# Reading a gate straight from PSUM, and writing each head's decay work in one piece, in a 25,527-instruction block kernel

## The reference, cut to what matters

```python
def second_block(x, ...):
    u = rmsnorm(h, norm_mix[l])                 # 272 tokens: 16 meta + 256
    proj = u @ w_in[l]                          # 1024 -> 6160 columns
    y_ssd = ssd_branch(z, xbc, dt_raw, ...)
    y_sc = short_conv_branch(gate_b, gate_c, h, conv_w, norm_g)
    h = h + jnp.concatenate([y_ssd, y_sc], axis=-1) @ w_out[l]
    ...                                         # router and experts

def short_conv_branch(gate_b, gate_c, h, conv_w, norm_g):
    v = causal_dwconv(gate_c * h, conv_w)
    return group_rmsnorm(gate_b * v, norm_g, SC_GROUPS)

def ssd_chunked(xs, dt, A, Bm, Cm):             # per head, chunks of 128 tokens
    seg = A_cum[..., :, None] - A_cum[..., None, :]
    Lmat = jnp.exp(jnp.where(causal, seg, -jnp.inf))
    CB = jnp.einsum('bcqgn,bckgn->bcgqk', Cc, Bc)
    y_diag = jnp.einsum('bcgqk,bcgrqk,bckgrp->bcqgrp', CB, Lmat, xdt)
    ...                                         # states carried over chunks, and y_off
```

## Time and profile before

| what | value |
|---|---|
| median of three runs | 1582.92 us |
| the profiled execution's own time | 1585.08 us |
| its span in the profile | 1583.3 us |
| PE busy | 1516.9 us (96%) |
| DVE busy | 847.7 us (54%) |
| ACT busy | 736.1 us (46%) |
| the chain that ended last | PE 79%, DVE 8%, DMA 5%, ACT 5% |
| the changed stage | about 1182 to 1285 us |

### The profile page before, as it was taken

How to read it: one execution, slowest core, us unless ns; L and a number is a source line. 1 busy time by engine, 2 the same in 40 slices (tenths; PEclk the granted TensorE clock), 3 DMA queues, 4 the chain that set the end, 5 groups by cost and what they waited for, 6 DMA issues and landing times.

```text
span 1583.3 us, 25527 instructions
## 1 busy us (share of the span) xinstructions
PE 1516.9 (96%) x10510; PEld 1175.5 (74%) x10510; DVE 847.7 (54%) x1494; ACT 736.1 (46%) x1151; POOL 1.4 (0%) x6
## 2 busy tenths in 40 slices
PE   8999989999999999999999999999999989999986
PEld 5645668777787778879968899997988889544442
DVE  2446666744333444674497765666578765212213
ACT  3535562543322332363364754546555644555444
POOL 0000000000000000000000000000000000000000
PEclk9999999999999999999999999999999999999999
DMA  9411633344433442343302446543444336999995
GB/s 388 174 44 64 209 128 106 133 160 160 163 117 133 159 175 103 135 159 108 107 1 84 157 154 206 186 147 135 159 143 152 110 145 251 421 420 421 421 420 226
DMA packets 42777, 288.29 MB, mean 182 GB/s; under 512 B 4880, under 2 KB 5008, under 8 KB 11808
## 3 DMA queue, kind: packets, MB, share of 16 engines
q1 hardware_dynamic: 42336, 285.93, 48.0%
q0 software_dynamic: 176, 0.59, 0.1%
q10 hardware_dynamic: 144, 0.06, 0.0%
HBM read 285.51 MB, written 1.05 MB: 181 GB/s over the span
## 4 chain that ended last, share of the span: by engine, by line
PE 79%; DVE 8%; DMA 5%; ACT 5%; issue 2%; SPq 1%; DVEq 0%; ACTq 0%
PE ps L550 16%; PE ps L551 16%; PE ps L552 16%; PE ps L3006 6%; DMA deep<-wts 5%; PE ps L601 2%; ACT WH L525 2%; DVE WL L535 1%; PE ps L1483 1%; PE ps L1581 1%; PE ps L1552 1%; DVE X L2126 1%; PE ps L2882 1%; PE ps L1653 1%; PE ps L1652 1%
## 5 line engine op out<-in xcount | busy, mean ns | idle before, releaser
L535 DVE TENSOR_TENSOR WL<-ring,WH 128x2048 fp32r<-128x2048 f32 (+2 forms) x134 | 281.2, 2103 | 138.7 <-ACT WH L525 138.6
L550 PE MATMUL ps<-HH,WH 128*128 128x512 f32 (+2 forms) x944 | 325.6, 345 | 3.6 <-DVE WL L535 3.6
L551 PE MATMUL ps<-HL,WH 128*128 128x512 f32 (+2 forms) x944 | 320.6, 340 | 0.0
L552 PE MATMUL ps<-HH,WL 128*128 128x512 f32 (+2 forms) x944 | 320.5, 339 | 0.0
L525 ACT ACTIVATE WH<-ring 128x2048 fp32r<-128x2048 f32 (+2 forms) x134 | 236.1, 1764 | 168.4 <-PE ps L552 91.4
L550 PEld LDWEIGHTS ps<-HH,WH 128*128 128x128 f32 (+1 forms) x944 | 179.1, 190 | 43.8 <-issue 19.3
L552 PEld LDWEIGHTS ps<-HH,WL 128*128 128x128 f32 (+1 forms) x944 | 179.1, 190 | 20.3
L551 PEld LDWEIGHTS ps<-HL,WH 128*128 128x128 f32 (+1 forms) x944 | 179.3, 190 | 18.4
L550 PE MATMUL ps<-UHL,WH 128*128 128x256 f32 (+3 forms) x416 | 121.8, 293 | 6.2 <-ACT cst L2351 2.4
L550 PE MATMUL ps<-parts,WH 128*128 128x512 f32 (+1 forms) x352 | 119.1, 338 | 0.4 <-DVE WL L535 0.4
L551 PE MATMUL ps<-UHL,WH 128*128 128x256 f32 (+3 forms) x416 | 118.3, 284 | 0.0
(11 more groups left out here) (425 smaller groups left out, 2508.2 us busy)
## 6 DMA issues: line engine op xcount, KB each, us to landing
ring<-wts SPq DMA_DIRECT2D x138, 1024.0 KB, 5.0
deep<-wts SPq DMA_DIRECT2D x80, 1024.0 KB, 18.2
ring<-wts SPq DMA_DIRECT2D x32, 704.0 KB, 4.0
under_x<-wts SPq DMA_DIRECT2D x12, 1024.0 KB, 19.9
arena<-wts SPq DMA_DIRECT2D x8, 1024.0 KB, 15.2
ring<-wts SPq DMA_DIRECT2D x4, 672.0 KB, 13.4
X<-xin SPq DMA_DIRECT2D x4, 512.0 KB, 16.2
ahead<-wts SPq DMA_DIRECT2D x2, 1024.0 KB, 8.1
```

Source lines behind the costliest of these rows:

```text
L535: e.tensor_tensor(lo, raw(i), hi.bitcast(F32), ALU.subtract).then_inc(*up("low", i))
L550: e.matmul(o, w[0][:, cols], x[0], start=k == 0, stop=False)
L551: e.matmul(o, w[0][:, cols], x[1], start=False, stop=False)
L552: return e.matmul(o, w[1][:, cols], x[0], start=False, stop=k == nk - 1)
```

## The change

It has four parts.

1. ACT's copy of part 0 (L2178) goes. The last of DVE's five operations on a short-convolution tile reads part 0 in its PSUM bank instead.
2. The bank of part 0 is therefore given back with that operation (`sc_out`, x, 4), and in the list it stands behind the bank of part 2. All later banks are handed out in another order.
3. DVE's near and mix of one head are written in one piece (`dve_head_decay`), so a step is near of head i, mix of head i, out of head i - 2.
4. In ACT's and DVE's programs the split of a chunk stood between scan 2i - 1 and scan 2i. It now stands ahead of scan 2i - 1, for the chunk before that one, so that each chunk's split comes one scan later than it did.

```diff
 def act_sc_tile(e, f):
     x, part = divmod(f, 3)
-    if part == 0:
-        e.wait_ge(*win_done(24 + f))
-        e.activation(YC[:, x, :], B("win", 24 + f)[:, LATENT], ACT.Copy).then_inc(*up("sc_gate.kept", x))
-    elif part == 1:
+    if part == 1:
...
 # dve_sc_tile, last operation
-e.tensor_tensor(YC[:, x, :], CV[:, z, LATENT], YC[:, x, :], ALU.mult).then_inc(*up("sc_out", x, 4))
+e.tensor_tensor(YC[:, x, :], CV[:, z, LATENT], B("win", 24 + f - 2)[:, LATENT],
+                ALU.mult).then_inc(*up("sc_out", x, 4))
...
-def dve_head_near(e, h):
+def dve_head_decay(e, h):
...
-    e.tensor_scalar(EZ[:, 528:656], second, bc(2, 128), 0.0, ALU.add, ALU.min).then_inc(*up("head_mixed.near", h))
-
-def dve_head_mix(e, h):
-    EZ = EE[h % 4]
+    e.tensor_scalar(EZ[:, 528:656], b[:, 144:272], bc(2, 128), 0.0, ALU.add,
+                    ALU.min).then_inc(*up("head_mixed.near", h))
     e.wait_ge(*at("head_exp", h))
...
 # dve_scan
-    i = f - 5
-    if i < 16:
-        dve_head_near(e, i)
-    if 0 <= i - 1 < 16:
-        dve_head_mix(e, i - 1)
-    if 0 <= i - 2 < 16:
-        dve_head_out(e, i - 2)
+    step_heads(f - 5, lambda h: dve_head_decay(e, h), lambda h: dve_head_out(e, h))
...
 # pe_second_half
-banks.give(banks.of["win", 24 + f], *(("sc_gate.kept", x), ("sc_gate", x), ("sc_out", x, 0))[part])
+if part == 1:
+    banks.give(banks.of["win", 24 + f], "sc_gate", x)
+elif part == 2:
+    banks.give(banks.of["win", 24 + f], "sc_out", x, 0)
+    banks.give(banks.of["win", 24 + f - 2], "sc_out", x, 4)
...
 def dve_second_half(e):          # act_second_half likewise
-    dve_low(e, index["win", 12])
-    dve_win_tile(e, 22)
-    dve_win_tile(e, 23)
     for i in range(12):
-        if i:
-            dve_scan(e, 2 * i - 1)
-        if i < 11:
-            dve_low(e, index["win", 13 + i])
-        dve_scan(e, 2 * i)
+        dve_low(e, index["win", 12 + i])
+        if i == 0:
+            dve_win_tile(e, 22)
+            dve_win_tile(e, 23)
+        for f in (2 * i - 1, 2 * i):
+            if f >= 0:
+                dve_scan(e, f)
     dve_scan(e, 23)
```

More of the change, by code:

```diff
@@ L2338, in head_bias @@
             return lambda i, n: bias6[0:n, 16 * i + h:16 * i + h + 1]
-        def head_decays(h):
-            return B("head", h)[:, 16:144], B("head", h)[:, 144:272]
         def act_head_decay(e, h):
             EZ = EE[h % 4]
-            (first, second), bc = head_decays(h), head_bias(h)
+            b, bc = B("head", h), head_bias(h)
             e.wait_ge(*at("head_mixed.near", h))
@@ L2348, in act_head_decay @@
                 e.wait_ge(*at("head_out", h - 4))
-            e.activation(EZ[0:16, 16:144], first[0:16, :], ACT.Exp, bias=bc(3, 16), scale=1.0)
-            e.activation(EZ[0:16, 144:272], second[0:16, :], ACT.Exp, bias=bc(4, 16), scale=1.0)
-            e.activation(EZ[:, 400:528], second, ACT.Exp, bias=bc(5, 128), scale=1.0).then_inc(*up("head_exp.far", h))
+            e.activation(EZ[0:16, 16:144], b[0:16, 16:144], ACT.Exp, bias=bc(3, 16), scale=1.0)
+            e.activation(EZ[0:16, 144:272], b[0:16, 144:272], ACT.Exp, bias=bc(4, 16), scale=1.0)
+            e.activation(EZ[:, 400:528], b[:, 144:272], ACT.Exp, bias=bc(5, 128),
+                         scale=1.0).then_inc(*up("head_exp.far", h))
             e.activation(EZ[:, 272:400], EZ[:, 272:400], ACT.Exp)
             e.activation(EZ[:, 528:656], EZ[:, 528:656], ACT.Exp).then_inc(*up("head_exp", h))
-        def dve_head_near(e, h):
+        def dve_head_decay(e, h):
             EZ = EE[h % 4]
-            (first, second), bc = head_decays(h), head_bias(h)
+            b, bc = B("head", h), head_bias(h)
             e.wait_ge(*at("decay_bias"))
@@ L2361, in dve_head_near @@
                 e.wait_ge(*at("head_out", h - 4))
-            e.tensor_scalar(EZ[:, 272:400], first, bc(1, 128), 0.0, ALU.add, ALU.min)
-            e.tensor_scalar(EZ[:, 528:656], second, bc(2, 128), 0.0, ALU.add, ALU.min).then_inc(*up("head_mixed.near", h))
-        def dve_head_mix(e, h):
-            EZ = EE[h % 4]
+            e.tensor_scalar(EZ[:, 272:400], b[:, 16:144], bc(1, 128), 0.0, ALU.add, ALU.min)
+            e.tensor_scalar(EZ[:, 528:656], b[:, 144:272], bc(2, 128), 0.0, ALU.add,
+                            ALU.min).then_inc(*up("head_mixed.near", h))
             e.wait_ge(*at("head_exp", h))
@@ L2481, in pe_second_half @@
                         pe_scan(e, f - 1)
-                    banks.give(banks.of["win", 24 + f], *(("sc_gate.kept", x), ("sc_gate", x), ("sc_out", x, 0))[part])
+                    if part == 1:
[3 more added lines that the diff above has]
+                        banks.give(banks.of["win", 24 + f - 2], "sc_out", x, 4)
             pe_scan(e, 23)
         def act_second_half(e):
-            act_high(e, index["win", 12])
-            act_win_tile(e, 22)
-            act_win_tile(e, 23)
             for i in range(12):
-                if i:
-                    act_scan(e, 2 * i - 1)
-                if i < 11:
-                    act_high(e, index["win", 13 + i])
-                act_scan(e, 2 * i)
+                act_high(e, index["win", 12 + i])
+                if i == 0:
+                    act_win_tile(e, 22)
+                    act_win_tile(e, 23)
+                for f in (2 * i - 1, 2 * i):
+                    if f >= 0:
+                        act_scan(e, f)
             act_scan(e, 23)
         def dve_second_half(e):
-            dve_low(e, index["win", 12])
-            dve_win_tile(e, 22)
-            dve_win_tile(e, 23)
             for i in range(12):
-                if i:
-                    dve_scan(e, 2 * i - 1)
-                if i < 11:
-                    dve_low(e, index["win", 13 + i])
-                dve_scan(e, 2 * i)
+                dve_low(e, index["win", 12 + i])
+                if i == 0:
+                    dve_win_tile(e, 22)
+                    dve_win_tile(e, 23)
+                for f in (2 * i - 1, 2 * i):
+                    if f >= 0:
+                        dve_scan(e, f)
             dve_scan(e, 23)
```

## The result

The changed kernel took 1593.96 us (median of 8 runs, 1589.9 to 1598.95) against 1584.0 (8 runs, 1580.3 to 1590.27) for the kernel before on the same chip. The ratio is 1.006 with a 95% interval of 1.0045 to 1.0077: slower by 0.6%, an estimated 7 to 12 us. The forecast was 1591.6 us, +8.7. The profiled execution of the changed kernel took 1596.89 us, its span is 1595.1.

A forecast was written before the change was run, and what follows sets the result against it. PE bounds the stage before; the change makes DVE the bound. Terms of -0.4, +7.5 and +1.6 give +8.7 us on 1582.9, so 1591.6 us; own range 1587 to 1595, 8 times in 10 1586.5 to 1597.

The forecast's parts named there:

- the forecast's mechanism: In the head steps DVE waits for ACT's exponentials between near and mix and becomes the bound; chance 0.76.
- Parts 1 and 2 cost nothing: DVE's last short-convolution multiply reading PSUM costs 0, later banks cost 0, and PE's 1.63 us stop at tile 3 goes.
- the wait of 1.42 a head: Between near and mix DVE waits 1.42 us per head; six scans take DVE 30.0 us against PE's 25.7.
- Part 4 uses slack in the middle: Later splits use only slack mid-stage; near the end the root comes earlier and one DVE split moves into the tail.
- first rival: The wait fits in DVE's air and PE's two stops go: 5.7 us won, 1577.2 us; chance 0.07.
- PE is stopped from tile 12: PE's first long stop is 1.9 us at column tile 12; from there PE follows DVE.
- It goes through to the end: What the stage gains or loses reaches the kernel's end, the expert stage keeping its length.
- second rival: The stage grows, but the experts' weight load at 420 GB/s takes it up: 1582.9 us; chance 0.05.
- third rival: PE's clock falls at about five new stops, 1.7 us each: +8.5 more, 1600.1 us; chance 0.12.
- The 1.7 us that the prediction read from the mean of 0.79: Loss from PE's slow clock over 8 us after the 2.39 us stop ahead of tile 23: 0.21 x 8 = 1.7 us.
- The sum: Along DVE's program: start -0.4, near 0 to near 15 +7.5, near 15 to output projection +1.6; together +8.7 us.
- bounds of -2.4 and +7: Effect on the sum over 16 heads if the wait between near and mix is at least 1.27 or at most 1.9 us.

The follow-up runs named there:

- two exponentials fewer: Changed kernel without ACT's last two exponentials of every head: 2733.87 us, including an expert branch at the end that the other kernels don't enter.
- out between near and mix: Changed kernel with out of head i - 2 placed between near and mix of head i on DVE: 1589.98 us, ratio 1.0021 against before.
- longer exponentials: Three of ACT's five exponentials per head split into halves, in the changed kernel (1597.7 us, ratio 1.0089) and in the kernel before (1584.98 us, 0.9999).
- part 3 alone: Kernel before with only near and mix of a head put in one piece on DVE: 1592.62 us, ratio 1.0057.
- DVE's splits as before: Changed kernel with DVE's splits back where they stood, ACT's still one scan later: 1602.46 us, ratio 1.0121 against before.
- parts 1 and 2 alone: Kernel before with only ACT's copy of part 0 gone and its bank given back later: 1585.68 us, ratio 1.0003.
- part 4 alone: Kernel before with only ACT's and DVE's splits one scan later: 1581.14 us, ratio 0.9986.
- ACT's half alone: Kernel before with only ACT's splits one scan later, DVE's program untouched: 1580.15 us, ratio 0.997.
- all but part 3: Changed kernel with near and mix of a head apart again, mix one step later: 1578.9 us, ratio 0.9972 against before.

## Why the prediction was right

Four kernels have DVE as the bound and a different sum of mix's waits:

| kernel | mix's waits, us | stage, us | difference of waits | of stage |
|---|---|---|---|---|
| changed | 23.6 | 117.60 | | |
| two exponentials fewer | 17.2 | 111.20 | -6.4 | -6.40 |
| out between near and mix | 17.7 | 111.66 | -5.9 | -5.94 |
| longer exponentials | 28.8 | 122.82 | +5.2 | +5.22 |

As long as DVE is the bound and nothing else moves, a microsecond of waiting is a microsecond of the stage. Two more kernels with DVE as the bound are not in the table because their splits stand elsewhere too: part 3 alone (23.2 us of waits, stage 118.23) and the one with DVE's splits as before (29.9 and 125.53). Where near and mix are apart, the stage is 104 to 109 us, and in the kernel before longer exponentials do next to nothing. The two together are the forecast's mechanism, shown from both sides.

By the steps of the prediction:

- **Parts 1 and 2 cost nothing.** Right: +0.4 us, ratio 1.0003. The multiply with its operand in PSUM takes 0.42 us in the changed kernel, as it did from SBUF. By the Trainium skill ("VectorE: DVE Perf Modes", the section on the TRN2 errata) the eight reads of PSUM came to an estimated +0.5 us, which for this stage can't be told from that +0.4, but the duration of the operation itself speaks against it. That the stop at tile 3 goes was right, but it stands under the wrong part: with parts 1 and 2 alone it stays at 1.61, with part 4 alone it goes. The reason given (`decay_bias` written ahead of a split of DVE) holds for the changed kernel: with DVE's splits where they were, the stop is back, and L2286 is its releaser.
- **Part 3, the wait of 1.42 a head, DVE the bound.** Right: 1.92 us from near to mix (1.94), six scans in 29.96 us (30.0). Near 0 to near 15 took 1281.59 - 1206.62 = 74.97 us (74.8), and near 15 to the first operation of the output projection 1296.85 - 1281.59 = 15.26 (15.2). The rows:

```profile
1206.62 0.34 DVE L2358 TENSOR_SCALAR arena<-ps,arena 128x128 f32<-128x128 f32 x1
...
1281.59 0.34 DVE L2358 TENSOR_SCALAR cst<-ps,arena 128x128 f32<-128x128 f32 x1
...
1284.72 0.41 DVE L2363 TENSOR_TENSOR cst<-cst,arena 16x256 f32<-16x256 f32 x1 [2.53 <-ACT cst L2349]
...
1296.85 0.32 DVE L2643 TENSOR_TENSOR vec<-vec 128x160 f32<-128x160 f32 x1
```

  Near 15 to its mix is 3.13 us (3.1), since the table load stands in it.
- **Part 4 uses slack in the middle.** True of DVE's half in the kernel before; ACT's half was given no size. In the kernel before, ACT's half alone is worth 4.7 us of stage: the stops at tiles 3 and 23 go. The prediction had the pieces of this in its first rival (1.6 + 2.4 + 1.7 = 5.7 us won), but it put the first of them under the banks and priced none of them as ACT's. In the changed kernel it isn't seen, because DVE sets the pace there. And DVE's half is not free in the changed kernel: it keeps the two splits side by side, without which the stage is 7.9 longer.
- **PE is stopped from tile 12.** Right in place and size: 1.97 us (1.9).
- **It goes through to the end.** Right: from the second output chunk to the end is 295.5 to 296.5 us in the kernels before, changed, and with one part or all but one, while their stages run from 104.0 to 118.2. The second rival (the weight load takes it up) is out.
- **The clock.** The third rival had its stops, and the clock did fall twice in the stage. After the stop ahead of tile 18 the first matmul took 0.55 us (the window 1203 to 1264 stands at 0.97), and tile 19 began 4.73 us after tile 18, where it was 3.27 in the kernel before, so PE lost 1.5 us. After the stop ahead of tile 23 the window from 1285 to 1300 stands at 0.89. It cost the stage nothing: from near 0 to the first operation of the output projection DVE never waits for PE, only for ACT, 23.6 us at mix and 0.74 at the root. The stop of 1.97 us at tile 12 was followed by a matmul of 0.36, full speed, so a stop of such a length does not by itself bring the clock down. The Trainium skill's rule that full clock can be taken back ("TensorE: Matmul & The Clock Gate", Part 1) agrees with tile 18. The 1.7 us that the prediction read from the mean of 0.79 in the kernel before was a little high: there PE took 4.46 us from its first matmul of tile 23 to the next work behind the tile, most of it at half speed, and with part 4 alone 3.07, a difference of 1.4.
- **The sum.** +8.55 us of stage against +8.7, and its three terms are right one by one, so no two errors cancel: near 0 came 0.7 us earlier after the start of the stage (-0.4 forecast), near 0 to near 15 grew by 7.6 (+7.5), near 15 to the output projection by 1.6 (+1.6). The range was not worked out as soundly: by the prediction's own bounds of -2.4 and +7 on 1591.6 it is 1589 to 1599, and for the stated 1587 to 1595 no working is given. The measured time lies in both. The median is 2.4 us above the forecast. 1.1 of it is the kernel before, 1584.0 in this comparison and 1582.9 in the three runs shown; the rest is within the interval.

## What to carry to other kernels

When one engine hands work to another and takes the result back, put other work of its own between the two; a wait in the queue costs its full length, once per step, from the point at which that engine's idle time is used up. To see it coming, compare pace with pace over one period (here six scans, 25.7 against 30.0 us) instead of adding busy times, whose sum hardly moves. And if such a wait can't be avoided, see what stands ahead of the answering operation on the other engine: here ACT's splits were free beside DVE's, and ahead of the exponentials they made mix's waits 6.3 us longer.

## What the runs showed of the hardware that I had not expected

Activations on 64 columns are not half as long as on 128: in the kernel with longer exponentials the starts of those that read PSUM lie 0.19 to 0.20 us apart (0.25 at 128 columns in the changed kernel), and four that read SBUF begin within 0.44 us, 0.15 apart (0.20 at 128). By these, eight for five are 2 x 0.195 - 0.25 + 4 x 0.147 - 2 x 0.20 = 0.33 us a head more, and 16 x 0.33 = 5.3 us is what the waits grew by (5.2).

```profile
1226.43 0.29 ACT L2346 ACTIVATE arena<-ps,arena 128x64 f32<-128x64 f32 x1
1226.62 0.29 ACT L2347 ACTIVATE arena<-ps,arena 128x64 f32<-128x64 f32 x1
1226.82 0.53 ACT L2350 ACTIVATE arena<-arena 128x64 f32<-128x64 f32 x3
1227.26 0.24 ACT L2351 ACTIVATE arena<-arena 128x64 f32<-128x64 f32 x1
```

The clock also falls in a part that no kernel here changes. In the window 1000 to 1100 us, first of before and then of the changed kernel:

```profile
1000.00:1100.00 100.00, 96.97 (x841) 91.70 (x840) 68.54 (x115) 52.09 (x79) 0.00 (x0) 1.00 0.42 141
```
```profile
1000.00:1100.00 100.00, 97.18 (x800) 89.66 (x799) 64.19 (x109) 49.47 (x76) 0.00 (x0) 0.93 0.40 136
```

It stood at 0.93 with parts 1 and 2 alone too, and at 1.00 with part 3 alone, part 4 alone and all but part 3. The start of the stage lay between 1175.1 and 1183.0 us over the twelve profiles, though nothing ahead of it differs but names and line numbers. The spread of the runs of one kernel goes with the clock. Of the 30 runs of the kernel before that stand beside the second set of experiments, four with a mean granted clock of 0.998 took 1580.6 to 1581.9 us, twelve with 0.994 took 1583.8 to 1587.4, and two with 0.990 took 1593.6 and 1593.7. What makes the clock fall more often in one run than in another stays open. A change of this size is better read inside the profile than from single times.
